# A two-layer mixer kernel on one core: first gate tile's weights, row squares and the norm's spread put elsewhere in the start

## What is computed

```python
h = rmsnorm(x, g)                      # x / sqrt(mean(x*x) + EPS) * g
p = h @ w_in                           # [hc | B | C | zA | q | k | v | zR | gA | gR]
a = ((b * conv) * silu(z_a)) @ w_a     # gated short convolution
r = (o * silu(z_r)) @ w_r              # retention, 4 heads
x = x + (sigmoid(g_a) * a + sigmoid(g_r) * r) @ w_o
```

## Time and profile before

| what | value |
|---|---|
| median of three runs | 2308.16 us (2308.12 to 2308.62) |
| the profiled execution | 2309.91 us, span 2308.1 us |
| PE busy | 2281.9 us, 99% |
| DVE, POOL, ACT busy | 60%, 39%, 38% |
| granted TensorE clock, mean | 0.997 |

### The profile page before, as it was taken

The page is one execution under the profiler, slowest core; times in us unless marked ns, Lnnn a source line. Parts: engine busy times, 40 slices in busy tenths (PEclk is TensorE's granted clock), DMA queues, the critical chain, the costliest instruction groups (busy, mean ns, idle before and its releaser), DMA issues.

```text
span 2308.1 us, 40644 instructions
## 1 busy us (share of the span) xinstructions
PE 2281.9 (99%) x17005; PEld 2260.2 (98%) x17005; DVE 1380.4 (60%) x1486; ACT 870.1 (38%) x1366; POOL 902.7 (39%) x603
## 2 busy tenths in 40 slices
PE   7999999999999999999999999999999999999998
PEld 7999999999999999999999999999999999999998
DVE  6676777556663565743475776774566536556434
ACT  6433333344444444322234333334334444333133
POOL 3555665565555300000036556555655651000000
PEclk9999999999999999999999999999999999999999
DMA  8221222244333565554452212223443335656444
GB/s 299 84 65 59 64 75 65 67 133 133 117 111 113 200 209 192 183 171 123 133 162 85 65 51 71 66 65 107 131 133 105 104 113 210 225 187 209 124 151 133
DMA packets 260519, 294.06 MB, mean 127 GB/s; under 512 B 9032, under 2 KB 218224, under 8 KB 260336
## 3 DMA queue, kind: packets, MB, share of 16 engines
q1 hardware_dynamic: 260176, 291.40, 39.1%
q10 hardware_dynamic: 160, 0.05, 0.0%
HBM read 206.84 MB, written 84.57 MB: 126 GB/s over the span
## 4 chain that ended last, share of the span: by engine, by line
PE 92%; issue 2%; DVE 2%; POOL 1%; DMA 1%; ACT 1%; SPq 1%; DVEq 0%; ACTq 0%; POOLq 0%
PE ps L1608 61%; PE ps L1650 21%; PE ps L1869 3%; DVE t_lo L1142 1%; PE ps L1659 1%; PE ps L1657 1%; PE ps L1658 1%; PE ps L1754 1%; PE ps L1699 1%; PE ps L1688 1%; DMA w_pair<-in_w_in_dram 1%; POOL s_lo L688 1%; PE ps L1597 0%; SPq L515 0%; DMA xs<-x_keep 0%
## 5 line engine op out<-in xcount | busy, mean ns | idle before, releaser
L1608 PE MATMUL ps<-t_hi,s_hi 128*128 128x272 f32 x3808 | 787.6, 288 | 5.9 <-DVE U L1156 4.1
L1608 PE MATMUL ps<-t_hi,s_lo 128*128 128x272 f32 x3808 | 788.2, 288 | 0.0
L1608 PE MATMUL ps<-t_lo,s_hi 128*128 128x272 f32 x3808 | 785.0, 288 | 0.0
L1608 PEld LDWEIGHTS ps<-t_hi,s_hi 128*128 128x128 f32 x3808 | 598.8, 188 | 6.7 <-DVE U L1156 4.5
L1608 PEld LDWEIGHTS ps<-t_lo,s_hi 128*128 128x128 f32 x3808 | 598.4, 189 | 0.0
L1608 PEld LDWEIGHTS ps<-t_hi,s_lo 128*128 128x128 f32 x3808 | 594.3, 189 | 0.0
L1175 DVE TENSOR_TENSOR e<-ps,snap 128x544 f32<-128x544 f32 x272 | 195.8, 722 | 518.6 <-PE ps L1608 391.1
L688 POOL TENSOR_TENSOR s_lo<-w_pair,s_hi 128x512 fp32r<-128x512 f32 x136 | 231.0, 1698 | 309.1 <-ACT s_hi L825 309.1
L835 ACT ACTIVATE snap<-ps 128x544 f32<-128x544 f32 x272 | 168.8, 621 | 433.8 <-PE ps L1608 433.4
L825 ACT ACTIVATE s_hi<-w_pair 128x512 fp32r<-128x512 f32 x204 | 127.5, 628 | 171.0 <-PE ps L1608 167.3
L699 POOL TENSOR_TENSOR sA<-w_pair 128x512 f32<-128x512 f32 x68 | 88.2, 1298 | 241.9 <-DVE s_lo L1163 220.3
(11 more groups left out here) (242 smaller groups left out, 3725.2 us busy)
## 6 DMA issues: line engine op xcount, KB each, us to landing
w_pair<-in_w_in_dram SPq DMA_DIRECT2D x136, 512.0 KB, 5.1
w_raw<-in_w_o_dram SPq DMA_DIRECT2D x24, 512.0 KB, 5.2
xs<-x_keep SPq DMA_DIRECT2D x16, 544.0 KB, 6.3
prod_keep<-e SPq DMA_DIRECT2D x16, 544.0 KB, 2.7
v_keep<-e SPq DMA_DIRECT2D x16, 544.0 KB, 7.2
z_keep<-e SPq DMA_DIRECT2D x16, 544.0 KB, 3.7
prod_raw<-prod_keep SPq DMA_DIRECT2D x16, 544.0 KB, 6.1
vT<-v_keep SPq DMA_DIRECT2D x16, 544.0 KB, 7.4
```

What stands on the lines that cost most here:

```text
L1608: i = mm(ps[:, r + p, 0:PART], s[j][:, k, :], b[operand][:, k, p * PART:(p + 1) * PART], start=(FRESH[j] and k == 0 and t == 0), stop=(k = ...
```

## The change

Five edits go together. (1) SP issues `load_unit(0, U_G)` behind the fourth chunk of x, and no longer behind the sample chunk; `load_unit(0, U_G + 1)` stays behind it. (2) ACT does four row squares between its four copies (one behind each copy's predecessor), where there were seven; the other five stand between the high parts of k = 0 to 4, one behind each k, where two stood behind k = 1 and 3. (3) DVE's `row_means` moves from behind k = 2 to behind k = 4 of `low_h`. (4) PE's `norm_spread` moves from ahead of k = 6 to ahead of k = 7 of gate tile 0. (5) POOL's split of gate tile 1 in layer 0 waits for six k of `low_h`, and no longer for eight. Layer 1 is as it was.

```diff
@@ sync
             sp.dma_start(ident[:, :], ident_c).then_inc(ident_loaded, 16)
-            for c in range(NCH):
-                sp.dma_start(x_rows[:, c, :], x_prompt[0, c * P:(c + 1) * P, :]).then_inc(rows_loaded[c], 16)
-            sp.dma_start(x1_t[0:DEC, 0:D], x_sample[0]).then_inc(rows_loaded[NCH], 16)
...
-            for idx in range(2):
-                load_unit(0, U_G + idx)
+            for c in range(NCH):
+                sp.dma_start(x_rows[:, c, :], x_prompt[0, c * P:(c + 1) * P, :]).then_inc(rows_loaded[c], 16)
+                if c == 3:
+                    load_unit(0, U_G)
+            sp.dma_start(x1_t[0:DEC, 0:D], x_sample[0]).then_inc(rows_loaded[NCH], 16)
+            load_unit(0, U_G + 1)
@@ gpsimd, split
-                    pool.wait_ge(act_ready, KT * (l + 1))
+                    pool.wait_ge(act_ready, KT * (l + 1) if l else KT - 2)
@@ scalar
             for c in range(NCH - 1):
-                square_rows(c)
                 if c % 2 == 0:
+                    square_rows(c // 2)
                     act.wait_ge(rows_turned, c + 1)
@@ scalar, layer 0
                         high_h(0, k, x[:, k, :])
-                        if k in (1, 3):
-                            square_rows(NCH - 1 + k // 2)
+                        if k < 5:
+                            square_rows(4 + k)
@@ vector, layer 0
                         low_h(0, k, x[:, k, :])
-                        if k == 2:
+                        if k == 4:
                             row_means()
@@ tensor, gate_unit
-                    if i_ == 0 and k == (7 if l else 6):
+                    if i_ == 0 and k == KT - 1:
                         norm_spread(l)
```

## The result

The changed kernel takes 2313.5 us (median of 14 runs, 2309.38 to 2315.5), the kernel before beside it 2308.19 us (14 runs, 2304.76 to 2312.63). The ratio is 1.0022, with a 95% interval of 1.0014 to 1.0029: 5.1 us **slower**, from 3.2 to 6.7. The forecast was 2309.0, with a range of 2306.6 to 2310.8 and 0.95 on no change. The measured time lies above that range.

The account below looks back on a forecast made before the run. The prediction took DVE's chain of combine, low and gate steps to bound the start. Of combine(0)'s 2.5 us delay, 0.8 us would arrive: 2308.16 + 0.8 = 2309.0 us, range 2306.6 to 2310.8.

Parts of the forecast that it names:

- What bounds the start: At the start, DVE's chain of combine, low and gate steps sets the end; PE finishes gate tiles 2.7 us earlier.
- The load and the copies: Start: earlier load removes PE's 3.2 us wait, chunk 8 lands 1.6 us later; T 20.3, PE's earlier start lost.
- T: Moment at which ACT starts the first high part: 20.62 us before, forecast 20.3, from 20.0 to 20.6.
- The squares, the means, the power, the spread's own place: Gate tile 0: power hidden, spread ends at T + 18.4 = 38.7 us, combine(0) starts at 41.2, 2.5 us later.
- PE has 2.7 us to spare for this: Gate tile 0's end: POOL's split may hold PE's last term; gate tile 1 starts 40.2 to 41.1, within slack.
- The split's end is a fixed point: DVE's chain at gate tile 2's split, ending 50.3: four combine(1) instructions behind it, not three; +0.7 us, not 1.65.
- The clock: Rival: the clock falls and stays at 1.2 GHz in gate tile 0; +5.6 us, 2313.8 us; chance 0.04.
- The sum: All of the delay that reaches the end: +0.8 us, between 0 and +1.7.

Follow-up runs that it names:

- e5: Changed kernel with DVE's gate 2 moved ahead of combine(3) in both layers; ratio to the kernel before 0.9999.
- e6: Kernel before with DVE's gate 2 moved ahead of combine(3) in both layers; ratio to the kernel before 0.9982.
- e4: Changed kernel with the weights of gate tile 0 loaded behind the sample chunk again; ratio to the kernel before 1.0009.
- e1: Changed kernel with POOL's split of gate tile 1 waiting for all eight low parts again; ratio to the kernel before 1.0004.
- e3: Changed kernel with squares and means back where they were, load, spread and POOL's wait still changed; ratio to the kernel before 1.0000.
- e2: Changed kernel with the spread ahead of k = 6 again; ratio to the kernel before 1.0006.
- e11: Changed kernel with the spread's place and POOL's wait undone, so only load, squares and means changed; ratio to the kernel before 1.0005.
- e7: Changed kernel with 24 unused matmuls on PE in its wait for DVE ahead of the first pair; ratio to the kernel before 1.0017.
- e10: Kernel before with only POOL's split of gate tile 1 waiting for six low parts; ratio to the kernel before 1.0001.
- e8: Changed kernel run once more without any edit; ratio to the kernel before 1.0015.

## Why the prediction was wrong, point by point

**What bounds the start: right.** The forecast said that DVE's chain sets the first pair and PE has slack. The wait for DVE stayed and grew, and moving gate 2 alone changed the end (e5, e6).

**The load and the copies: right, with some luck in the number.** T 20.17 for 20.3, PE's start 21.71 for 21.7, the gain lost in gate tile 0. Chunk 8 landed at 17.06 (forecast 17.2) and T followed 3.11 us behind it (3.1). The terms written out for this, 1.0, 1.23 and 0.69, add up to 2.9; the rest is in the gaps between them. A repeat need not come so near: T ranged from 19.49 to 21.24 in kernels that are alike up to there. That the load order changes nothing of the start is seen in e4's profile alone; the timed runs leave it open.

**The squares, the means, the power, the spread's own place: right in size.** The forecast put the spread's end at T + 18.4 and combine(0) at T + 20.9. With edit 5 undone (e1) they are at T + 18.48 and T + 20.88.

**"PE has 2.7 us to spare for this": the first step that failed.** The forecast saw that POOL's early split would put DVE's low parts of k = 6 and 7 behind, but booked it on PE's last term of gate tile 0 and on gate tile 1 alone. The low part of k = 6 is also ahead of the spread, since the spread had moved behind k = 6. It ended at 37.06, 0.6 us behind POOL's w_hi, so the spread was late: T + 19.86 instead of T + 18.4, and combine(0) came 3.77 us later than before, not 2.5. The forecast for a low part beside a split, some 0.6 us behind POOL's end, would have given most of this, had it been followed to the spread. The Trainium skill, "SBUF — State Buffer", Who interferes with whom, says that a DVE instruction with two inputs in SBUF contends with a POOL instruction that reads SBUF, and that the order of issue decides who is blocked. The traces agree that the two block each other: the six low parts took 8.01 us beside POOL's split and 4.27 without it, and in e3 it was POOL's w_hi that took 4.41 instead of 1.89 us. On the order of issue they do not all agree as far as start times tell it: the changed kernel's w_hi (34.16) came ahead of the low part it held (34.64), but in e3 w_hi began at 32.21, ahead of the last three low parts, and all three still ran first.

**"The split's end is a fixed point": the second step that failed.** It forecast that of the delay of combine(0) only 0.7 to 0.8 us would reach the pair, as one DVE instruction more stands behind the split of gate tile 2. In e1 it would have held: its combine(0) is 1.71 us later than in the kernel before and its pair 0.58. In the changed kernel neither part of it did. The two splits came later themselves, by 0.6 and 1.8 us. And DVE meets the first of them a whole step earlier, with low(0), of which POOL's two instructions hold the last two: 6.52 us instead of 2.63. It then meets the next split with combine(1) instead of low(1). Before, the steps from combine(0) to low(1) lost 0.8, 3.2 and 3.8 us to splits, 7.8 in all; after, low(0) lost 3.9 and combine(1) 3.7, so 7.6. The loss moves along the chain and hardly shrinks: 3.58 of 3.77 us arrive. The size of the delay does not decide this. The same steps lost 6.7 us in e1 and 6.5 in e2, where w_lo of gate tile 2 fell beside gate 0, which reads PSUM and took its usual 1.00 us there: 1.71 us became 0.58, 3.27 became 2.05. In e11 they lost 8.2 (1.6 of it in combine(0), beside the split of gate tile 1), and a delay of 0.68 us became 1.03.

**The clock: the right fear in the wrong place.** The rival put the fall of the clock into gate tile 0, where PE's gaps are under 1 us; it did not outlast the second k there (it was back at 1.00 by 26 us). So it is luck that this rival's number, 2313.8, lies next to the measured 2313.5. What was not priced is that a later DVE lengthens PE's wait to 4.5 us, and that the pair then runs at 1.2 GHz from its first matmul on: 1.09 us in the profiles (e7). A wait of the length that the kernel before has, 2.7 us, may already do it: there the clock stayed up in the one profile, but with waits of 2.2 to 2.9 us it fell in e1, e2, e3 and e10.

The sum as it stands: 3.58 + 1.08 = 4.66 us at the ninth combination, against 5.1 us (3.2 to 6.7) in the timed runs; the forecast had 0.8. The profiles do not account for the timed difference as a whole, since layer 1 took 1.9 us of the 4.66 back in them; whether it does so in the timed runs is open.

## What to carry to other kernels

An instruction that is moved earlier on one engine can hold up those of another, so follow each instruction that it delays to everything that stands behind it on the third engine, in the new order and not in the old. Where a chain meets another engine's work on its way, how much of a delay arrives depends on which of its instructions stand beside that work; work out the step at which it meets them for the chain as it was and for the delayed one. When PE waits for a chain on another engine, look first for a product in that engine's order that can be delivered earlier: one line, gate 2 ahead of combine(3), gave 4 us here, where five edits ahead of it lost 5.

## What the runs showed that was not expected

The length of PE's wait ahead of the pair does not tell alone whether the clock falls. Behind 4.5 us it stood at 0.50 from the pair's start (changed, e8, e4), behind 2.9 us from the start or nearly so (e10, e3); behind 2.3 and 2.2 us (e1, e2) it fell 1 to 2 us into the pair; behind 2.2 us (e11) and 2.7 us (before) it did not fall. From the pair to the ninth combination the profiles without a fall have 53.35 to 53.36 us, e1 to e3 53.66 to 53.75, the changed kernel, e8 and e4 54.35 to 54.45, and e10 54.96. What decides it was not settled.

T differed from profile to profile by more than the edits move it: 19.49, 19.59, 19.90, 19.99, 20.17, 20.97 and 21.24 in kernels whose programs are the same up to there. The landing of chunk 8 sets it, and it varies: T follows it by 3.1 to 3.3 us in all seven.

Layer 1 has the same wait for gate 2 at its own start. In the profiles of the kernel before, e1, e2, e4, e10 and e11 PE lost 2.2 to 2.6 us there (1.3 to 1.7 for gate 2, then 0.9 for ACT's snap), in those of the changed kernel, e3, e7 and e8 0.2 to 0.4, and with gate 2 moved also 0.2 to 0.3. Whether that changes from run to run of one kernel, which would account for some 2 of the 8 us by which the runs of the kernel before differ, or goes with the kernel, was not settled: each kernel left one profile.
